# Picks in expert order, fetched during the last experts and summed in four strips of 32 tokens

## The reference

```python
N_EXPERTS = 64; TOP_K = 6; D_MODEL = 1024
_, eidx = lax.top_k(jnp.where(emask > 0, sel, -jnp.inf), TOP_K)
w = jnp.take_along_axis(scores, eidx, axis=-1)
w = w / jnp.sum(w, axis=-1, keepdims=True) * ROUTED_SCALE
...
return jax.ops.segment_sum(yb * row_w[:, None], row_tok, num_segments=T)
...
ffn = routed_experts(h2d, eidx, ew, w_exp_gate, w_exp_up, w_exp_down) + swiglu(h2d, w_sh_gate, w_sh_up, w_sh_down)
return layer_norm(DEEPNORM_ALPHA * h + ffn.reshape(B, L, D), ln2_g, ln2_b)
```

## Time and profile before

| | |
|---|---|
| median of 3 runs | 1809.27 us (1804.94 to 1813.5) |
| the profiled execution: its time | 1811.97 us |
| its span, first to last instruction | 1809.8 us |
| mean granted TensorE clock | 0.988 |
| busy: PE, DVE, ACT, POOL | 1740.8, 1069.2, 678.6, 331.7 us |
| DMA over the span | 409.01 MB, 226 GB/s |
| last expert product of TensorE ends | about 1717.7 us |
| first row of the end phase asked for | 1723.5 us |

### The profile page before, as it was taken

The page is one execution under the profiler, slowest core; times in us unless marked ns, Lnnn a source line. Parts: engine busy times, 40 slices in busy tenths (PEclk is TensorE's granted clock), DMA queues, the critical chain, the costliest instruction groups (busy, mean ns, idle before and its releaser), DMA issues. The chain is left out here.

```text
span 1809.8 us, 27145 instructions
## 1 busy us (share of the span) xinstructions
PE 1740.8 (96%) x9472; PEld 1336.0 (74%) x9472; DVE 1069.2 (59%) x1724; ACT 678.6 (37%) x1092; POOL 331.7 (18%) x282
## 2 busy tenths in 40 slices
PE   9999999999999999999996889999999999999996
PEld 9999999999955555998873556767676767676633
DVE  3112442634345565745684657777777777777568
ACT  3112222312244555212110145656565656565411
POOL 0000321412010000000145332222222222222112
PEclk9999999999999999999997999999999999999998
DMA  6332633434223123624260589999999999999697
GB/s 223 93 93 76 169 118 108 145 118 136 74 67 102 40 67 136 244 83 156 92 239 1 181 293 374 394 379 404 396 407 382 398 393 384 397 396 366 226 376 315
DMA packets 140736, 409.01 MB, mean 226 GB/s; under 512 B 29444, under 2 KB 91300, under 8 KB 121060
## 3 DMA queue, kind: packets, MB, share of 16 engines
q1 hardware_dynamic: 116436, 338.38, 50.8%
q0 software_dynamic: 21344, 52.59, 7.6%
q10 hardware_dynamic: 2880, 17.04, 2.3%
HBM read 359.78 MB, written 67.80 MB: 236 GB/s over the span
## 5 line engine op out<-in xcount | busy, mean ns | idle before, releaser
L2675 PE MATMUL e_Y<-mixT,e_aT 128*128 128x512 f32 x544 | 246.7, 596 | 6.8 <-issue 5.8
L2686 PE MATMUL e_G<-w_lo,xT_hi 128*128 128x512 f32 x528 | 205.7, 390 | 0.0
L2675 PEld LDWEIGHTS e_Y<-mixT,e_aT 128*128 128x128 f32 x544 | 103.5, 191 | 112.1 <-issue 107.0
L2533 DVE TENSOR_TENSOR w_lo<-wb,e_w_hi 128x1024 fp32r<-128x1024 f32 x132 | 155.5, 1220 | 16.4 <-ACT e_w_hi L2453 9.5
L2526 DVE TENSOR_TENSOR xT_lo<-e_T,xT_hi 128x1024 fp32r<-128x1024 f32 x66 | 80.8, 1225 | 133.3 <-ACT xT_hi L2448 133.3
L2533 DVE TENSOR_TENSOR w_lo<-wb,half_hi 128x1024 fp32r<-128x1024 f32 x128 | 150.7, 1220 | 10.4 <-ACT half_hi L2453 10.2
L1323 PE MATMUL banks<-x_hi,gw_hi 128*128 128x352 f32 x464 | 151.6, 327 | 1.4 <-DVE r_srg L1115 1.4
L1323 PE MATMUL banks<-x_hi,gw_lo 128*128 128x352 f32 x464 | 148.8, 321 | 0.0
L1323 PE MATMUL banks<-x_lo,gw_hi 128*128 128x352 f32 x464 | 148.8, 321 | 0.0
L2448 ACT CAST xT_hi<-e_T 128x1024 fp32r<-128x1024 f32 x66 | 67.1, 1017 | 206.8 <-PE e_T L2664 206.8
L187 PE MATMUL banks<-w_hi,x_hi 128*128 128x244 f32 x512 | 142.0, 277 | 1.6 <-DVE x_lo L244 1.6
(11 more groups left out here) (436 smaller groups left out, 3604.2 us busy)
## 6 DMA issues: line engine op xcount, KB each, us to landing
wb<-in_w_exp_gu SPq DMA_DIRECT2D x64, 2048.0 KB
mixT<-in_w_exp_dn SPq DMA_DIRECT2D x68, 1024.0 KB
yk<-d_y_rows SPq DMA_DIRECT2D x16, 1536.0 KB, 18.9
gw_sb<-in_w_gate SPq DMA_DIRECT2D x20, 512.0 KB, 7.0
d_proj<-o_sb SPq DMA_DIRECT2D x8, 1098.0 KB, 5.6
d_gateT<-r_g_out ACTq DMA_DIRECT2D x16, 528.0 KB, 2.6
pages<-in_cache_both SPq DMA_DIRECT2D x64, 128.0 KB, 2.0
wb<-in_w_exp_gu ACTq DMA_DIRECT2D x4, 2048.0 KB
```

Source lines behind the costliest of these rows:

```text
L2533: v.tensor_tensor(w_lo[s][:, :, at_k, :], w_gu[s][:, :, at_k, :], w_hi[c][:, :, at_k, :].bitcast(F32), ALU.subtract).then_inc(w_lo_ok, 1)
L2675: mm = t_.matmul(Y[q][:], aT[:, c, k, :], w_d[:, s, k, q * 512:(q + 1) * 512], start=k == 0, stop=k == 1)
L2686: mm = t_.matmul(G[c], x[:, c, k, :], w[:, :, k, :], start=k == 0 and i == 0, stop=k == KD - 1 and i == 2)
```

## The change

1. **Picks by expert number.** After the top-six the trunk casts the indices to float in a field of eight (the last two are -1) and sorts them with one more `max` for each tile. Pick 0 is now the highest expert number, picks 4 and 5 the lowest two. The weights follow.
2. **Order of blocks.** The four overflow blocks run before experts 60 to 63, not after them. At most four picks of a token are among these four experts, so picks 4 and 5 are always written before them.
3. **Loads.** Each tile has a buffer `pair` for picks 4 and 5 (128 rows x 8 KB), asked for while the last four experts run, in memory that expert weights leave. `acc` of tiles 0 and 1 lies in `early` and is loaded in the trunk; gain and bias of the norm are loaded late.
4. **Stacks.** Picks 0 to 3 of a tile go into a `stack`: partition 32 x pick + (token mod 32), and q = token div 32 along the row. They are asked for by `stack(t, j)`, two picks at a time (j = 1: picks 2 and 3; j = 0: picks 0 and 1), in four DMAs, one for each q. Each DMA's destination is 64 partitions x 4 KB; its source has the dimensions 2 (pick, step 4 KB), 32 (token, step 32 KB) and 1024 elements, in this order. There are 64 such DMAs of 256 KB.
5. **Sum.** TensorE multiplies, for each q and each half c of the row, a [128 x 32] matrix `w_stack` with the stack, into partitions 32q to 32q + 31 of S: eight matmuls for a tile, and all four picks in one. VectorE adds picks 4 and 5, two instructions for a tile, eight in all before or between the last experts' work and eight after. Tile 8 comes last.

```diff
-LAST_ORDER = (NT - 1, *range(NT - 1))
+LAST_ORDER = range(NT)
...
-                link(v.tensor_copy(f6[:].rearrange("p (t k) -> p t k", k=TOPK), i8[:, :, 0:TOPK]))
+                link(v.tensor_copy(f8[:, :, 0:TOPK], i8[:, :, 0:TOPK]))
+                for t in range(G):
+                    ins = v.max(by_number[:, t, :], f8[:, t, :])
+                link(ins)
+                link(v.tensor_copy(f6[:].rearrange("p (t k) -> p t k", k=TOPK), by_number[:, :, 0:TOPK]))
...
+            def pair(t):
+                sp.dma_start(pairs[t][:].rearrange("p k n -> p (k n)"),
+                             y_rows.rearrange("(t k) n -> t (k n)", k=8)[t * P:(t + 1) * P, 4 * D:6 * D]).then_inc(pair_in[t], 16)
+            def stack(t, j):
+                b = stack_of[t][0]
+                for q in range(4):
+                    sp.dma_start(stacks[b][2 * NS * j:2 * NS * (j + 1), q, :],
+                                 y_rows.rearrange("(t k) n -> t k n", k=8)[t * P + NS * q:t * P + NS * (q + 1), 2 * j:2 * j + 2, :].rearrange("t k n -> k t n")).then_inc(stack_in[b], 16)
...
+            weights_read(0)
+            rows_written(NE - W)
+            pair(0)
+            pair(1)
...
+            rows_written(NE - W + 2)
+            stack(0, 1)
+            weights_read(3)
+            stack(1, 1)
+            stack(2, 1)
...
+            rows_written(NE)
+            stack(0, 0)
+            stack(1, 0)
...
+            sp.wait_ge(pe_done, 1)
+            stack(7, 1)
+            stack(7, 0)
+            h_tile(NT - 1)
+            for k in range(TOPK):
+                small(k)
             for i, t in enumerate(LAST_ORDER):
-                if i + 4 < NT:
-                    sp.wait_ge(pe_done, i + 1)
-                    rows_of(i + 4, 0)
-                    sp.wait_ge(joined, i + 1)
-                    rows_of(i + 4, 1)
                 sp.wait_ge(out_ok, i + 1)
...
+                    if last and s in (1, 2):
+                        quarters((2 * s - 2, 2 * s - 1))
...
+                    if last and s == W - 2:
+                        small_weights()
+                    if last and s == W - 1:
+                        for t, k in ((0, 5), (1, 4), (1, 5)):
+                            add_row(t, k)
                     gated(at(dve, r, W, s + 1), c)
+                    if last and s == 1:
+                        add_row(0, 4)
...
             def routed(i):
                 t = LAST_ORDER[i]
-                pe.wait_ge(diag_ok, t // 3 + 1)
-                pe.wait_ge(yk_in[i % 4], at_buffer(i))
-                for k in range(ON_PE):
-                    for c in range(2):
-                        mm = t_.matmul(S[i % 4][:, c, :], diag[:, t, k, :], yk[i % 4][:, k, c * 512:(c + 1) * 512], start=False, stop=k == ON_PE - 1)
+                b, use = stack_of[t]
+                pe.wait_ge(stacked_ok, 1)
+                pe.wait_ge(stack_in[b], 128 * use)
+                for c in range(2):
+                    for q in range(4):
+                        mm = t_.matmul(S[i % 4][NS * q:NS * (q + 1), c, :], w_stack[:, t, q, :], stacks[b][:, q, c * 512:(c + 1) * 512], start=False, stop=True)
                 mm.then_inc(pe_done, 1)
```

More of the change, by code:

```diff
@@ L2242, in _, with experts @@
             mm.then_inc(e_gu_done, 1)
[L2245 removed]
+def experts(nc, passed, begun, parts, acc_in, acc, pair_in, pairs, stack_in, stacks, w_stack, small_rows, junk, shared, ident, wb, gu_in, ready, w_d, d_in, ln2, ln2_in, a, h_rows, tok_list, meta, y_rows, out_p, out_s):
     with ExitStack() as ctx:
@@ L2349, in h_tile @@
+            r = sp.snap(more + (NE // W - 1))
+            for s in range(W):
+                refill(r, s, NE - W + s)
             def h_tile(t):
                 n = P if t < NT - 1 else NS
[L2351 to L2360, removed]
@@ new lines, in pair_added @@
+            def pair_added(t):
+                sp.wait_ge(added, 2 * t + 2)
+            weights_read(0)
+            rows_written(NE - W)
+            pair(0)
+            pair(1)
+            wait_alone(sp, x_turned, sp.snap(more * (2 * W) + 2 * (NE - W + 2)))
+            pair(2)
+            weights_read(1)
+            pair(4)
+            pair(5)
+            down_read(0)
+            h_tile(2)
+            h_tile(3)
+            wait_alone(sp, x_turned, sp.snap(more * (2 * W) + 2 * NE))
@@ new lines, in _ @@
+            pair(3)
+            weights_read(2)
+            pair(6)
+            pair(7)
+            down_read(1)
+            h_tile(4)
+            h_tile(5)
+            rows_written(NE - W + 2)
[3 more added lines that the diff above has]
+            stack(2, 1)
+            down_read(2)
+            h_tile(6)
+            h_tile(7)
+            pair_added(1)
+            stack(3, 1)
+            pair_added(3)
+            stack(4, 1)
+            rows_written(NE)
@@ new lines, in add_row @@
+            def add_row(t, k):
+                assert (t, k) == (n_added[0] // 2, 4 + n_added[0] % 2)
+                if t not in tile_added:
+                    dve.wait_ge(acc_in[t], 16)
+                else:
+                    dve.wait_ge(added, tile_added[t])
+                dve.wait_ge(pair_in[t], 16)
+                v.scalar_tensor_tensor(acc[t][:], pairs[t][:, k % 2, :], w_part[:, t, k:k + 1], acc[t][:], ALU.mult, ALU.add).then_inc(added, 1)
+                n_added[0] += 1
+                tile_added[t] = n_added[0]
@@ L2758, in _ @@
             shared_down(2)
-            for i in range(NT):
-                if i == 0:
+            routed(0)
+            routed(1)
+            for i in range(2, NT):
+                if i < NT - 1:
+                    routed(i)
+                else:
                     routed_small()
-                else:
-                    routed(i)
-                if 1 <= i and i + 3 < NT:
-                    shared_down(i + 3)
+                if i + 2 < NT:
+                    shared_down(i + 2)
 def program(nc, a, o):
```

197 lines of the change are left out of this document (116 added, 81 removed).

## The result

The changed kernel takes 2070.54 us (median of 4 runs, 2066.12 to 2075.53), the kernel before 1807.27 us (4 runs, 1804.94 to 1813.50): a ratio of 1.146, with a 95% interval of 1.143 to 1.149. Forecast were 2075 us, 2030 to 2140.

A forecast was written before the change was run, and what follows sets the result against it. The end phase was taken as three nearly equal loads: TensorE 8.58 us a tile, VectorE about 7.7, DMA 7.4 plus output. Start 1719, stacks 332, other DMAs 7.5 and tail 17.7 gave span 2076, time 2075 us, range 2030 to 2140.

The forecast's parts named there:

- Two engines for a stack DMA, the same two for all: Stack loads: the source's outermost count of 2 confines all 64 DMAs to one pair of engines; chance 0.86.
- 332 us for the stacks: End phase: 64 stack DMAs of 32 packets per engine at 162 ns queue up on two engines.
- the forecast's start of 1719: Stack start: eight pairs and four tiles of h, queued from 1694, take 24.6 us at 427 GB/s.
- The landing of a scatter: Before the first stack is asked for: block 66's scatter lands 4.11 us after 1705.37, at 1709.5.
- The tail: After the last input at 2058.5: landing, small tile's matmuls at possibly half clock, and 8.8 to the end; 17.7 us.
- Three microseconds for the steps pulled in: Before the experts end: VectorE's pulled-in additions and ScalarE's small copies cost 3 us, bounds 1 to 6.
- 1.5 for choosing: Third batch in the trunk: the cast and three max that sort picks cost 0.5 to 5 us, taken as 1.5.
- Strips: TensorE's stack sums: four strips run beside each other, sixteen instructions a tile in 1.8 us instead of 5.15.
- Rival C: TensorE's stack sums: DMAs spread, but strips of one bank don't overlap, 6.86 us a tile; 1817 us; chance 0.02 with others.
- rival A: Stack loads: DMAs spread over all 16 engines at 427 GB/s; 1779 us, 30 faster; chance 0.08.

The follow-up runs named there:

- e3: Changed kernel with all four picks of 32 tokens in one stack DMA (32 DMAs of 128 rows, outermost source count 4): 1904.94 us.
- e1: Changed kernel with the stack DMAs' source read token first (outermost count 32), so weights do not fit the rows: 1821.15 us, 1.011 of the kernel before.
- e4: Changed kernel with half of its stack DMAs (picks 0 and 1) asked for on ScalarE's queue: 2067.95 us.
- e7: The kernel before, unchanged, run once more for a profile on another chip: 1794.95 us.
- e8: The kernel before with only the sorting of picks by expert number added: 1794.49 us, ratio 1.0008 to the kernel before.
- e6: e5 with the weights built to fit its spread rows, everything computed: 1775.41 us, 0.992 of the kernel before.
- e9: e6 with the wait for the last rows and three stacks of picks 0 and 1 moved earlier: 1774.22 us, 0.989 of the kernel before.
- e12: The kernel of e9 once more, on one chip with a repeat of e6: 1773.39 us, 0.9903 of the kernel before.
- e5: e1 with each stack DMA's 64 rows sent to every second partition, weights again not fitting: 1773.70 us, 0.990 of the kernel before.
- e10: e1 with stack DMAs alternating between partitions 64 to 127 and 0 to 63 from tile 2 on, weights not fitting: 1814.15 us.

## Why the prediction was right, point by point

**Two engines for a stack DMA, the same two for all: right.** It was the step on which nearly all of the slowdown rests. The small packets show it (2 for each DMA, 4 in e3), the share (0.128, 0.256), and e1, in which one altered order of dimensions takes 239 us out of the end phase. e3 and e4 exclude the two rivals to it, a fixed number of engines and a limit of the queue.

**332 us for the stacks: right, with the row 4% too dear and the start too early.** A row took 156 ns, not 162: 64 x 32 x 0.156 = 319 us. The first stack was asked for at 1716.22 (forecast 1714), the last landed at 2054.71; the forecast had the last packets, those of the small rows, at 2058.5. From the forecast's start of 1719 to 2053.2 (1.5 us before the landing) there are 334 us, of which the stacks and the 32 rows asked for ahead of the last of them (h, gain, bias) explain 319 + 5. Of the other 10 us two parts can be seen. The stacks began later: from 1690 to 1724 us SyncE's queue (q1) moved 10.61 MB and GpSimd's (q0) 1.33. 10.49 MB of the first are the pairs and the h, so the stacks had had 0.12 MB by 1724, two or three us' work of two engines: they began near 1722 and not at 1719. The 1.33 MB of GpSimd's queue are its scatters, which the forecast did not count in the queue ahead of the stacks. And the last tile came 42.3 us after the one before it, where that one took 39.9. Some 5 us stay untraced.

**That the sum fits within 5 us is in part luck.** The rows were 12 us too dear in all, and the 10 us above were missing; these nearly cancel. The landing of a scatter was mis-sized too: 4.11 us in the forecast, 8.75 for block 66 here (1707.39 to 1716.14). The 4.11 us were read from block 68 of the kernel before, an overflow block with hardly a row in it. In that trace GpSimd's queue has 144 packets and 0.00 MB from 1719.3 to 1724 us. The change puts four experts at the end, whose scatters carry rows (the 1.33 MB above) and run beside the pairs; which of the two makes the landing longer was not separated. The scatter itself came 2.5 us sooner than forecast (1707.39 against 1709.9), which hid half of that.

**The tail: its size right, its parts not.** From 2054.71 to the end there are 17.4 us, forecast 16.2 behind the landing. The forecast had 7.4 us for the small tile's matmuls at half the clock. They took 4.2, but the last full tile's strips, which the forecast left out, stand between the landing and them and took 3.4: 7.6 in all, by luck. From the last join to the end of the span 9.6, forecast 8.8.

**Three microseconds for the steps pulled in: right. 1.5 for choosing: not refuted.** TensorE turned the last block's rows 3.05 us ahead of the kernel before (1690.51 against 1693.56) and began the last gate-and-up product at the same moment (1703.20 against 1703.19): 3.06 us lost. The row of the first addition shows where:

```profile
1695.34 1.28 DVE L2664 SCALAR_TENSOR_TENSOR early<-pair,e_w_part,early 128x1024 f32<-128x1024 f32 x1 [4.75 <-DMA pair<-d_y_rows]
```

VectorE waited 4.75 us for pair 0 with the splits of the last expert behind it. The experts were over at 1717.5, as in the kernel before (1717.7), and not near 1722, only because all of them stood 3 us earlier in this execution; e7 shows that such shifts occur without any change. Choosing cost 1.4 us in e8, with an interval that holds 0 as well as 1.5.

**Strips: right.** 1.92 us for sixteen instructions in e6 at the full clock, forecast 1.8; 3.64 in the changed kernel, forecast 3.6 for 1.2 GHz. Rival C, strips that don't overlap and 6.86 us a tile, is excluded.

**What the prediction missed.** First, that SyncE is held at each issue; it cost nothing that can be seen, since e4, where SyncE hands out half of the stacks, has the same end phase to 0.2 us. Second, the half rate: rival A, "spread over all 16 engines, then 1779", rested on 427 GB/s from the earlier trace rows, a row of loads over 128 partitions, and the stacks write 64. With sixteen engines alone the kernel is slower than before, 1.011 in e1, and a reader who trusted rival A would have mended one fault and found no gain. Even with both mended, rival A's 30 us were 14 to 20 (ratios 0.992 to 0.989): the end phase is 74 us and not the 61 that 1779 means (less 1717.7). e6 shows where the difference lies. Rival A had TensorE work 35 us without a gap behind the four shared products; it took 50 (1714.84 to 1764.88). The two waits for stacks make 11.9 of the 15, and the first two tiles, at the lower clock in part, most of the rest. The DMA engines are full from 1676 us on in e6, well ahead of these waits, so the stacks come as the full queue lets them, at 363 GB/s from 1700 to 1710 and some 410 after that, and not at 427 from the start. Asking sooner for some of them (e9, e12) only moved the waits.

## What to carry to other kernels

- Look at the outermost dimension of both sides of a DMA before its bytes. A `rearrange` that puts a short dimension outermost can leave 2 of 16 engines. The number of small packets for each DMA tells how many there are, and the DMA share in the stretch tells it again.
- A full DMA share is not a full rate. Read GB/s beside it: 1.03 at 213 GB/s and 1.03 at 410 were the same rows, sent to 64 neighbouring partitions or to every second one.
- Before a duration is carried over from the old trace, see how many bytes it moved: the 4.11 us of a nearly empty scatter became 8.75 when an expert's rows stood in its place.
- When one fault is mended, measure again before crediting the rest of the idea: here the second fault hid behind the first, and alone it turns a gain of 1% (e5) into a loss of 1% (e1).

## What the runs showed of the hardware

- With 2, 4 and 32 as the outermost count of the source, a DMA of SyncE went to 2, 4 and 16 engines (small packets for each DMA: 2, 4, 16; the changed kernel, e3, e1). DMAs in flight together shared the same two (share 0.128).
- One row of 4 KB takes an engine 156 ns with two engines at work; two engines move 52 GB/s, four 105.
- SyncE can be held at an issue: from the fourth stack on, with some five in flight, each took it 4.8 us; with two queues on the same engines (e4) 9.6 us each; with sixteen engines at the full rate (e6) 0.6 us. DMAs behind it that would use all engines (h, gain, bias) come late too: the gain was asked for at 1849.65 us, in e6 at 1718.39.
- 64 partitions get 410 GB/s if they are every second one of 128 (e5), and 213 if they are neighbours (e1); alternating two halves from DMA to DMA gives 240 (e10).
- A scatter of GpSimd that moved 0.00 MB took 4.11 us to its landing (block 68 of the kernel before); one of an expert's rows, beside the pairs, 8.75 us (block 66 of the changed kernel).
- The same kernel reached its first turn of expert rows at 1001.1 us in one execution and at 1019.5 in another, with the end phase equal to 0.1 us (e7). What makes the difference stays open; the medians above point at the chip.
